# The first half of the layer projection moved from the routing to the last item but one, unread products put at the routing's waits, and the second half of the expert bias put ahead of the wait for the tokens

## The reference, cut to what matters

```python
def reference(x, p, ...):
    ...
    x = x + jnp.concatenate([fox_out, rwkv_out], axis=-1) @ w_out[i]
    x = x + moe_ffn(rmsnorm(x, moe_norm[i]), w_router[i], b_router[i], w_gu[i], b_gu[i],
                    w_down[i], b_down[i])
    gate = jax.nn.sigmoid(rmsnorm(x, ple_norm[i]) @ w_ple_gate[i])
    x = x + gate * (p[i] @ w_ple_proj[i])
return rmsnorm(x, final_norm)

def moe_ffn(...):     # per token: top 4 of 32 logits, softmax over the four
    ...
    hh = (xb @ w_gu[e] + b_gu[e]).astype(jnp.float32)
    glu = jnp.minimum(hh[:, :EXPERT_FF], SWIGLU_LIMIT)
    lin = jnp.clip(hh[:, EXPERT_FF:], -SWIGLU_LIMIT, SWIGLU_LIMIT)
    act = (glu * jax.nn.sigmoid(SWIGLU_ALPHA * glu) * (lin + 1.0)).astype(xt.dtype)
    return (act @ w_down[e] + b_down[e]).astype(jnp.float32) * gt[:, None]
```

## Time and profile before

| | |
|---|---|
| runs (3) | median 1198.6 us, 1197.23 to 1200.29 us |
| the profiled execution | 1198.85 us, its span 1197.1 us |
| TensorE busy | 1139.1 us, 95% of the span |
| VectorE, ScalarE busy | 24%, 14% |
| DMA | 434.90 MB, mean 363 GB/s |
| mean granted clock of TensorE | 0.997 |

### The profile page before, as it was taken

How to read it: one execution, slowest core, us unless ns; L and a number is a source line. 1 busy time by engine, 2 the same in 40 slices (tenths; PEclk the granted TensorE clock), 3 DMA queues, 4 the chain that set the end, 5 groups by cost and what they waited for, 6 DMA issues and landing times.

```text
span 1197.1 us, 16918 instructions
## 1 busy us (share of the span) xinstructions
PE 1139.1 (95%) x7060; PEld 482.6 (40%) x7060; DVE 282.5 (24%) x576; ACT 170.9 (14%) x317; POOL 0.2 (0%) x4
## 2 busy tenths in 40 slices
PE   7999999999999999999999999999999999999997
PEld 6888866533333333333333333333333332333334
DVE  2455635321111111112112111111111111111123
ACT  3323422211000000000110000000000000000014
POOL 0000000000000000000000000000000000000000
PEclk9999999999999999999999999999999999999999
DMA  9732125579999999999999999999999999999970
GB/s 372 320 141 73 38 107 212 228 297 400 428 428 427 428 429 429 429 429 428 429 428 428 429 429 428 427 429 429 429 429 428 429 428 429 429 429 429 425 312 36
DMA packets 32228, 434.90 MB, mean 363 GB/s; under 512 B 3840, under 2 KB 4096, under 8 KB 5952
## 3 DMA queue, kind: packets, MB, share of 16 engines
q1 hardware_dynamic: 32192, 434.37, 86.4%
HBM read 433.31 MB, written 1.05 MB: 363 GB/s over the span
## 4 chain that ended last, share of the span: by engine, by line
DMA 43%; PE 40%; ACT 0%; DVE 0%; issue 0%; SPq 0%; DVEq 0%
DMA ring<-in_we 42%; PE PS L855 27%; PE PS L940 2%; PE PS L703 2%; PE PS L817 2%; PE PS L832 2%; PE PS L869 1%; PE PS L824 1%; PE PS L899 0%; PE PS L753 0%; DMA hT<-in_wproj 0%; PE PS L879 0%; PE PS L759 0%; PE PS L498 0%; PE PS L840 0%
## 5 line engine op out<-in xcount | busy, mean ns | idle before, releaser
L855 PE MATMUL PS<-ring,FV 128*64 128x512 f32 x2304 | 515.4, 596 | 25.5 <-DMA ring<-in_we 25.5
L855 PEld LDWEIGHTS PS<-ring,FV 128*64 128x64 f32 x2304 | 158.1, 137 | 364.0 <-issue 302.7
L855 PE MATMUL PS<-B,FV 128*64 128x512 f32 x768 | 174.0, 595 | 9.4 <-DMA B<-in_we 8.7
L855 PEld LDWEIGHTS PS<-B,FV 128*64 128x64 f32 x768 | 53.0, 137 | 114.4 <-issue 98.6
L486 PE MATMUL PS<-hT,ring 128*128 128x256 f32 x416 | 93.0, 382 | 0.8 <-ACT hT L993 0.6
L486 PEld LDWEIGHTS PS<-hT,ring 128*128 128x128 f32 x416 | 78.1, 190 | 12.2 <-ACT hT L993 0.8
L1474 DVE TENSOR_SCALAR rz<-con,lora 64x64 f32<-64x64 f32 x30 | 7.4, 247 | 306.1 <-PE PS L855 306.1
L1556 DVE TENSOR_SCALAR hT<-PS 128x512 f32<-128x512 f32 x32 | 22.1, 692 | 185.1 <-PE PS L855 185.1
L1247 DVE TENSOR_TENSOR FV<-PS,prm 128x512 f32<-128x512 f32 x32 | 22.1, 692 | 183.8 <-PE PS L824 183.8
L817 PE MATMUL PS<-xq,rz 128*64 128x512 f32 x256 | 62.0, 605 | 0.0
L1152 ACT ACTIVATE FV<-PS 128x512 f32<-128x512 f32 x32 | 19.1, 597 | 297.8 <-PE PS L899 297.8
(11 more groups left out here) (266 smaller groups left out, 675.3 us busy)
## 6 DMA issues: line engine op xcount, KB each, us to landing
ring<-in_we SPq DMA_DIRECT2D x144, 2048.0 KB, 23.9
B<-in_we SPq DMA_DIRECT2D x48, 2048.0 KB, 29.3
ring<-in_wz SPq DMA_DIRECT2D x7, 2048.0 KB, 22.8
ring<-in_wo SPq DMA_DIRECT2D x2, 2048.0 KB, 8.1
ring<-in_wgate SPq DMA_DIRECT2D x2, 2048.0 KB, 38.8
xq<-in_x SPq DMA_DIRECT2D x2, 512.0 KB, 5.3
ring<-in_wz SPq DMA_DIRECT2D x1, 1024.0 KB, 8.5
xq<-in_x SPq DMA_DIRECT2D x1, 1024.0 KB, 4.8
```

The lines of the kernel that those rows point to most:

```text
L855: mm = pe.matmul(PS[64 * h:64 * h + 64, bank_, :], lhs(4 * (q % 2) + k), w[:, k, h, :], start=(first and k == 0), stop=(q % 2 == 1 and k = ...
```

## The change

Edit 1: `project` leaves the routing. It now stands in item `2 * last_pair`, the last but one: `project(0)` behind the product of q 4, `project(1)` behind that of q 5, both into bank 5, with the two copies to `PP` as new steps of ScalarE, whose loop ends an item pair earlier so that this item is written out. The weights' DMA goes to the place of `h2T` in `B`, behind the last piece of item 0, and waits for the logits (`lg1`).

Edit 2: `keep_busy(n)` runs n products of the identity with the first 512 columns of `xs` into bank 3, which nobody reads. There are six: one behind the logits, one behind the products that read `sel0`, two behind `rank`, one behind `gather(1)`, one behind `turn(1)`.

Edit 3: an item's bias products of `s` = 1 (bank 7) come first and no longer wait for `xT`; those of `s` = 0 do.

```diff
             sp.wait_ge(s_pe, pe_at["xo11"])
-            sp.dma_start(wproj0.rearrange("p k n -> p (k n)"), t["wproj"][0]).then_inc(s_ple, 16)
             first_item(5)
+            sp.wait_ge(s_pe, pe_at["lg1"])
+            sp.dma_start(wproj0, t["wproj"][0].rearrange("p (k n) -> p k n", k=2)).then_inc(s_ple, 16)
...
+            def project(b):
+
+                if b == 0:
+                    pe.wait_ge(s_ple, 32)
+                else:
+                    pe.wait_ge(s_projsb, 1)
+                for k in range(2):
+                    mm = pe.matmul(bank(5), pTt[:, k, b * P:(b + 1) * P], wproj0[:, k, :], start=(k == 0), stop=(k == 1))
+                mm.then_inc(s_proj, 1)
...
+            def keep_busy(n):
+
+                for _ in range(n):
+                    pe.matmul(bank(3), ident, xs[:, 0, 0:PW], start=True, stop=True)
+
+            pe.wait_ge(s_dve, dve_at["xo11"])
+            keep_busy(1)
             pe.wait_ge(s_dve, dve_at["sel0"])
             pe.matmul(PS[:, 4, 0:NE], c_("tri"), R[:, 2, :], start=True, stop=True)
             pe.matmul(PS[:, 4, NE:2 * NE], c_("ones")[:, 0:P], R[:, 2, :], start=True, stop=False)
-            pe.wait_ge(s_ple, 32)
-            project(0, 0)
-            project(0, 1)
+            keep_busy(1)
             pe.wait_ge(s_dve, dve_at["sel1"])
             fin(pe.matmul(PS[:, 4, NE:2 * NE], c_("tri"), R[:, 3, :], start=False, stop=True), "rank")
-            project(1, 0)
...
-            def item(i, odd, first=False, last=False):
+            def item(i, odd, first=False, last=False, projecting=False):
+                def bias(side):
+                    for h in range(2):
+                        rows = slice(NE * side, NE * side + NE)
+                        pe.matmul(PS[64 * h:64 * h + 64, 6 + side, :], OHB[rows, :], bT[rows, 512 * h:512 * h + 512],
+                                  start=True, stop=False)
+
                 pe.wait_ge(s_ohb, i + 1)
+                bias(1)
                 pe.wait_ge(s_xT, i + 1)
-                for h in range(2):
-                    for s in range(2):
-                        pe.matmul(PS[64 * h:64 * h + 64, 6 + s, :], OHB[NE * s:NE * s + NE, :],
-                                  bT[NE * s:NE * s + NE, 512 * h:512 * h + 512], start=True, stop=False)
+                bias(0)
...
                 product(i, odd, 4, 4, act_of, True)
+                if projecting:
+                    pe.wait_ge(s_gt, i + 1)
+                    project(0)
                 if not last:
                     turn(i + 2)
                 product(i, odd, 5, 4, act_of, False)
-
+                if projecting:
+                    project(1)
+
+            keep_busy(2)
             gather(1)
-            project(1, 1)
+            keep_busy(1)
             turn(1)
             pe.wait_ge(s_bt, 16)
+            keep_busy(1)
             item(0, False, first=True)
...
-            item(2 * last_pair, False)
+            item(2 * last_pair, False, projecting=True)
```

More of the change, by code:

```diff
@@ L95 @@
 PE_STEPS += [f"{kind}{n}" for kind, n in MIX_ORDER if kind not in ASIDE]
-PE_STEPS += ["mean", "var", "xo00", "xo01", "T00", "xo10", "T01", "xo11", "T10", "lg0", "T11", "lg1", "pp0", "rank", "pp2",
+PE_STEPS += ["mean", "var", "xo00", "xo01", "T00", "xo10", "T01", "xo11", "T10", "lg0", "T11", "lg1", "rank",
              "rrT", "grT", "count", "pos", "ri", "gi", "ei"]
@@ L137 @@
              + [f"z{n}" for n in range(10, 18)] + mixa
-             + ["gsd", "sq00", "sq01", "rx0", "sq10", "T10", "sq11", "T11", "rx1", "lex", "pp0", "pp2", "grT"])
+             + ["gsd", "sq00", "sq01", "rx0", "sq10", "T10", "sq11", "T11", "rx1", "lex", "grT"])
 def fox_rwkv7_moe_ple(nc, t, out):
@@ L216, in fox_rwkv7_moe_ple @@
         gate, junk = ring[:, 0, 0:2 * D], ring[:, 1, :]
-        wproj0 = hT[:, :, :].rearrange("p a b -> p (a b)")[:, 0:2 * PW].rearrange("p (k n) -> p k n", k=2)
+        wproj0 = B[:, 12:14, PW:D]
         wproj1 = LZ[:, :, :].rearrange("p a b -> p (a b)"), lora[:, 0:PW]
@@ L272, in fox_rwkv7_moe_ple @@
         s_used = sem("expert_pieces_used")
+        s_proj = sem("layer_projection_done")
+        s_projsb = sem("layer_projection_in_sbuf")
         s_sel = sem("selection_built")
@@ L776, in overflow_rows @@
             def overflow_rows():
-                pe.wait_ge(s_act, act_at["pp2"])
                 pe.wait_ge(s_dve, dve_at["rr"])
@@ L877, in gate_matrix @@
                     pe.wait_ge(s_glu, i + 1)
+                    if last:
+                        pe.wait_ge(s_projsb, 2)
                     for b in range(TB):
@@ L1132, in projected @@
             def projected(b):
-                pe_done(f"pp{2 * b}")
-                fin(act.activation(PP[:, b, 0:PW], bank(2 + b), ACT.Copy), f"pp{2 * b}")
+                act.wait_ge(s_proj, b + 1)
+                act.activation(PP[:, b, 0:PW], bank(5), ACT.Copy).then_inc(s_projsb, 1)
             def gathered(n):
@@ L1138, in gathered @@
                 act.activation(Xg, bank(6), ACT.Copy).then_inc(s_xg, 1)
-            projected(0)
-            act.wait_ge(s_act, act_at["pp0"])
             gathered(1)
-            projected(1)
             act.preload_act_table(ACT.Sigmoid)
@@ L1146, in _, with item @@
             fin(act.activation(GRT, PS[:, 3, 0:SEQ], ACT.Copy), "grT")
-            def item(i, last=False):
+            def item(i, last=False, projecting=False):
                 act.wait_ge(s_glu, i + 1)
@@ L1154, in item @@
                     gathered(i + 2)
+                if projecting:
+                    projected(0)
                 act.wait_ge(s_used, 6 * i + 6)
                 act.activation(ysb, bank(4), ACT.Copy).then_inc(s_ysb, 1)
+                if projecting:
+                    projected(1)
             item(0)
             act.wait_ge(s_dve, dve_at["tabs"])
-            last_item = act.value_load(EI[0:1, NITEM + 1:NITEM + 2], min_val=NE - 1, max_val=NITEM - 1)
-            with act.Fori(1, last_item) as i:
+            pairs = act.value_load(EI[0:1, NITEM + 2:NITEM + 3], min_val=NE // 2 - 2, max_val=NITEM // 2 - 2)
+            last_pair = pairs + 1
+            with act.Fori(1, 2 * last_pair) as i:
                 item(i)
-            item(last_item, last=True)
+            item(2 * last_pair, projecting=True)
+            item(2 * last_pair + 1, last=True)
             def fin_t(ins, name):
@@ L1604, in gated @@
                 v.wait_ge(s_tpe, tpe_at["pl1"])
+                v.wait_ge(s_projsb, 2)
                 fin_t(tt(sig, p, sig, ALU.mult), f"gp{g}")
```

## The result

| | runs | median us | lowest to highest |
|---|---|---|---|
| before | 20 | 1200.13 | 1196.96 to 1203.58 |
| changed | 20 | 1203.48 | 1199.06 to 1205.82 |

The ratio is 1.0024, with a 95% interval of 1.0015 to 1.0033: by it the change costs 2.9 us (the two medians differ by 3.35). That is less than the 0.3% that I had set as the bound of telling, but with 20 runs it is told. The profiled execution took 1204.26 us, its span is 1202.4. One later execution of the changed kernel (in f1) took 1984.21 us at a mean granted clock of 0.557; it is left out of every comparison.

A forecast was written before the change was run, and what follows sets the result against it. The saturated weight stream was taken as the bound: its start, its bytes over its rate, then TensorE's tail. Start -1.3, end +3.2, edit 3 and DMA 0 gave +1.9 us on median 1198.6: 1200.5, range 1197.3 to 1203.0.

The forecast's parts named there:

- The reference: The time of the kernel before to which the difference was added: median 1198.6 us.
- The start, -1.3 us: From the logits' end to item 0's first piece: the new order at full clock brings that piece 1.3 us earlier.
- The walk: Routing steps added up in the new order at full clock from 230.70, putting item 0's first piece at 240.49 us.
- the rival in which it falls: Behind the logits the clock still falls, 3.4 us at half speed: the change costs +3.6, 1202.2 us; chance 0.22.
- X: How much earlier item 0's first piece begins: 1.26 us at full clock, -0.4 if the clock falls.
- The tail, +3.2 us: Four projection products in the last item but one cost 3.82 us, 0.59 covered by a DMA wait, 3.23 paid.
- The absorbed rival: At the end, the projection hides in waits, so 3.23 vanishes and -1.3 stays: 1197.3 us; chance 0.10.
- the two groups of L761: Profile sign at the end: `project` in two groups of 1.9 us, 13 to 20 us ahead of the last item's q 2.
- The bias halves, 0: Edit 3, bias order in each item: worth 0, at most 0.1 us, if the four products still run together.
- The moved DMA, 0: The 0.5 MB weights' transfer behind item 0's piece 5: costs nothing, 1.2 us at most if in the way.
- The saturated stream: Weight DMA at about 428 GB/s: its start, set by item 0's first piece, moves every later issue and the last landing equally.

The follow-up runs named there:

- f1: The changed kernel repeated unchanged for a second profile; ratio 1.0014 to the kernel before.
- e5: The changed kernel with the projection's two calls moved ahead of q 2 and q 3 of the last item but one, into the DMA waits; ratio 1.0006 to before.
- e2: The changed kernel with the projection and its two copies in item 1 instead of the last item but one; ratio 0.9993 to the kernel before.
- e6: e2 with the first unread product moved from behind the logits to between the logits of the two token blocks; ratio 0.9980 to the kernel before.
- e7: e6 with one instead of two unread products behind the ranks; ratio 0.9974 to the kernel before.
- f2: The changed kernel with the first unread product moved between the two blocks' logits, projection left in the last item but one; ratio 1.0009 to before.
- f4: The kernel of e7 repeated unchanged; ratio 0.9982 to the kernel before.
- f3: e6 with only the moved unread product kept and the other five left out; ratio 1.0015 to the kernel before.
- e1: The kernel before, routing and projection untouched, with four unread products of the projection's size added in the last item but one; ratio 1.0022 to before.
- c0: The kernel before, repeated unchanged as control for spread and clock; ratio 0.9994.
- e4: The kernel before with edit 3 alone, the bank 7 bias products ahead of the wait for the tokens; ratio 1.0001.
- e3: The changed kernel without its six unread products; ratio 1.0036 to the kernel before.

## Why the prediction was wrong, and where it was right

I forecast 1200.5 us and no difference that can be told; measured was 1203.48, outside my range, and +0.24%. Two steps failed, the start's condition (that the clock stays up) and the reference, and the tail's term was a little too large.

- **The reference.** I put the difference on the median of three runs, 1198.6. Twenty runs of the same kernel have 1200.13. That is 1.5 of the 3.0 us between forecast and result. The three runs and the profile were too few for a kernel whose executions differ by the clock's low stretch; I had seen the 3.1 us of spread and not asked what made it.
- **The start, -1.3 us.** The walk was right for a start at full clock, as e5 shows: 240.44 against 240.49. Its condition was wrong. That the clock stays up from the logits on I took as likeliest, and the rival in which it falls got 0.22. In three of the four profiles of this routing (the changed kernel, f1, e2; not e5) it fell, and over 55 runs 23 are at 0.996 or under. I sized the rival at X = -0.4, and it came out at -0.3 counted from the logits' end. Over the executions the start is worth 0.8 us (e2, 0.9993), with an interval from 2.3 us gained to 0.6 lost.
- **What the start was compared with.** My -1.3 set a start at full clock against a profile of before that has 3.4 us at the lower level in it, but executions of before also run without. At the same mean clock the gain is gone: at 0.999 the changed kernel (its 20 runs and f1's) has a median of 1199.88 us in 10 runs against 1196.84 in 7 before; at 0.996 and under 1203.88 in 15 against 1200.68 in 63. That is 3.0 and 3.2 us more, about the tail's price alone. What the routing gives is fewer runs with a low clock. These groups are small and sorted after the fact, so they are a reading and no test.
- **Why the clock falls.** The reason that I gave for the rival, the same small products just ahead of the fall, is what e6 bears out: with one large product between them and four or five others behind, no run of 41 (e6, e7, f2, f4) is at 0.996 or under. f3 shows that the one alone does not do it. In e6 the product also left its place behind the logits, and no run puts other work of the same length within the logits, so that it is their small size that counts is argued, not shown. The Trainium skill (TensorE: Matmul & The Clock Gate, Part 1) says that the moment of a switch differs from run to run. The traces agree: the clock fell 0.6 us behind the end of the logits in the profile before and 0.1 behind it in the changed kernel's, and the same kernel has runs at 0.995 and at 0.999.
- **The tail, +3.2 us.** Right in place and mechanism, 2.87 measured; 3.68 for the four products instead of 3.82, and 0.81 given back instead of 0.59: the wait of 0.59 is counted from the end of the product before it, but the three pieces, from start to start, are 0.81 shorter without it. e1 alone gives 1.0022. The absorbed rival falls. One sign was misread in the prediction: by its own rows the two groups of L761 stand 16 and 10 us ahead of the last item's q 2, not 13 to 20, and they stand there in the trace.
- **The bias halves, 0.** Right: 1.0001, and the group at 1.02 in the loop. The rule of the Trainium skill (TensorE: Matmul & The Clock Gate, Part 3), that a weight load overlaps with running products only when its row group differs, does not hold for such pairs here: the group takes 1.02 us in either order.
- **The moved DMA, 0.** Nothing in any trace waited for it.
- **The saturated stream** as the frame: right in the main. Between item 0's first piece and the q 3 of the last item but one it is 868.84 us before and 869.05 to 869.14 in c0, e1, e2, e6 and f2, though their starts lie up to 3.2 us apart; e4, f1, f4 and the changed kernel had 869.56, 869.67, 870.26 and 871.28, and e3 and f3, whose first piece ran at the lower level, 871.66 and 870.54. So single executions differ here by as much as the change costs.

By the ratios the parts, tail (e1) and start (e2), sum to 1.0022 x 0.9993 = 1.0015 against 1.0024 and 1.0014 measured in two sets; the intervals overlap. With the right reference and the clock fallen, the prediction's own terms give 1200.1 + 3.6 = 1203.7.

## What to carry to other kernels

A wait for a transfer hides only work that is put ahead of it and behind the wait before, not work that stands behind it: the same four products cost 2.87 us behind the waits, 1.06 in them, and nothing in item 1, where TensorE lives on a store of pieces while the stream is saturated. Unread products paid here only as far as they kept the clock up. The clock fell at the end of the logits' small products, ahead of the waits that were filled, though TensorE had no pause in them (busy for all of 226 to 230 us in every profile), so the first unread product belongs inside that stretch. And before a difference of 0.2% is forecast, the spread of the reference should be taken apart by the mean clock of each run; one profile is one draw.

## What the runs showed of the hardware that I had not expected

- The low stretch after the logits has two lengths in the profiles, 3.4 and 6.8 us, and in f3 (3.4 and 3.4) and e3 (6.8 and 3.4) it comes twice with a time at full clock between. The kernel before had 3.4 us in one profile and 6.8 in another.
- In one profile (e7) a late piece made TensorE wait 2.33 us instead of 1.24 near the end, the clock fell 1.2 us into the piece behind the wait, and that piece took 5.35 us instead of 3.65, so a late transfer cost more than its lateness:

```profile
1110.45 5.35 PE L866 MATMUL PS<-ring,FV 128*64 128x512 f32 x16 [2.33 <-DMA ring<-in_we]
```
